# The sums of squares at six stage entries: summed by GpSimd in SBUF, or by TensorE in PSUM

## The chip, the core and the metric

The kernel runs on one core of a Trainium2 chip. The metric is the device time of one execution in microseconds (us), as the median of several. Lower is better. Everything is float32. TensorE (PE in the profile) multiplies, GpSimd (POOL), VectorE (DVE) and ScalarE (ACT) work elementwise, and the SP queue issues the weight DMAs.

## The reference, cut to what matters

The model is a chain of blocks on `x`, 512 tokens of width 1024: a mixer (convolution and attention), an MLP, a conformer convolution, a second MLP, and then a layer of another kind (forgetting attention and a gated feed-forward part). Six of its stages begin in the same way, with a root-mean-square norm of the running `x`, and a product of the normed `x` with a weight:

```python
def rms_norm(x, g):
    xf = x.astype(jnp.float32)
    y = xf * lax.rsqrt(jnp.mean(xf * xf, axis=-1, keepdims=True) + EPS)
    return (y * g.astype(jnp.float32)).astype(x.dtype)

for i in range(DEPTH):                       # DEPTH = 2
    h = rms_norm(x, g[0])                    # entries x0 (i = 0) and x2 (i = 1)
    m = parallel_conv_mla(h, ...) if i % 2 == 0 else conformer_conv(h, ...)
    x = x + rms_norm(m, g[1])
    h = rms_norm(x, g[2])                    # entries x1 and x3
    x = x + rms_norm(squared_relu_mlp(h, mlp_w1[i], mlp_w2[i]), g[3])
# second layer kind: n1 = _rmsnorm(h, norm1_w) is entry x4, n2 = _rmsnorm(h, norm2_w) is entry x5
```

## The kernel before

**Layout.** `x` lies transposed in SBUF: `X[:, k]` is k-tile k, 128 of the 1024 features on the partitions and the 512 tokens along the free dimension, k = 0 to 7. A float32 product is made of three products of fp32r parts: ScalarE rounds an operand to a high part (`XH`, `wh`), and another engine subtracts that from the original to get the low part (`XL` on VectorE, `wl` on GpSimd). `products` issues three matmuls: high x high, high x low, low x high. A weight block holds 8 tiles of 128x128 in a ring of 4 blocks; its chain is DMA, ScalarE `hi`, GpSimd `lo_range`, TensorE.

**The norm is applied afterwards.** A stage multiplies its weight with gain times `X`, not yet normed. Each output tile is multiplied with `r2`, the row of 1/rms factors of the 512 tokens, when VectorE takes it out of PSUM. So the products of an entry can start as soon as the first k-tile of the new `X` is there, and the factor is only wanted later. No output tile of a stage leaves PSUM before `r2` is ready, and TensorE can run four output tiles ahead at most (four PSUM banks, `bank_free`).

**An entry on TensorE** (`enter`, line 1475). The first three output tiles, t = 0 to 2, are computed together, one k-tile at a time: for each k TensorE waits for `xh` and `xl` of that k-tile, and issues 9 matmuls of 512 columns. (Entry x0 takes k = 0 to 3 for t = 0, then for t = 1, then for t = 2, and is k by k from k = 4.) Then comes the fourth output tile, t = 3, with two hooks: `stat` ahead of its k = 1 and `spread` ahead of its k = 5. `stat` (line 1433) sums the squares over the partitions: for each of four groups of 128 tokens it takes that 128x128 piece of `ssq` as the stationary operand and one column of ones as the moving one. These are float32 matmuls, which the profile shows as two each: 8 weight loads and 8 matmuls of one column. ScalarE takes the root (`root`, line 585), VectorE the reciprocal (`factor`), TensorE spreads it over the partitions (`spread`), and ScalarE copies it to `r2` (`keep_r2`).

**An entry on ScalarE** (`operand`, line 598). For each k: wait for the new `X[:, k]`, write `XH[:, k]` (line 610), then the square of `X[:, k]`: for k = 0 into `ssq` (line 614), for k >= 1 into `sqb[:, k % 2]` (line 619). The square of k-tile k waits until GpSimd has added that of k - 2, since it goes into the same half of `sqb`. ScalarE's queue is in order, so `XH[:, k + 1]` stands behind that wait, and the first weight block that is rounded after the entry stands behind all of them.

**An entry on VectorE** (`operand`, line 935). At x1 to x4, for each k: `update(k)` makes the new `X[:, k]` in two operations, and then `split(k - 1)` makes `XL[:, k - 1]`, once `XH[:, k - 1]` is there. At x0 and x5 `X` is there already, and only the splits are done.

**An entry on GpSimd** (`add_squares`, line 455). For k = 1 to 7 it waits for the square and adds `sqb[:, k % 2]` to `ssq` (line 462). This stands in GpSimd's one queue between two low parts of weight blocks: at x0 between the blocks 2 and 3, at the others behind the fourth block of the stage.

**Weight blocks around the entry.** The first four blocks of a stage are in the ring before the entry begins (at x0 the first three and, behind the additions, the fourth). Block 4 can be rounded when the first output tile is done with its block.

Of the kernel before, what the change touches and what calls it, by code (L numbers as in the profile page):

```python
# [31 lines left out]
P = 128  # L32
# [63 lines left out]

SSQ_ADDS = [sum(t - (name[0] == "x") for name, t, _ in _JOBS[:i + 1]) for i in range(len(_JOBS))]
JOB_D = [d for _, _, d in _JOBS]
# [30 lines left out]
def build(nc, x_t, meta_t, positions, vectors, weights, out_t):  # L129
    ctx = ExitStack()  # L130
    with ctx:
# [133 lines left out]
        xl = sem("xl")  # L265
        squares = sem("squares")
        ssq_adds = sem("ssq_adds")
        stat_done = sem("stat_done")
# [135 lines left out]
        def _(pool):  # L404
# [49 lines left out]

            def add_squares(entry):

                before = SSQ_ADDS[JOB[entry]] - (KT - 1)
                for k in range(1, KT):
                    pool.wait_ge(squares, SQUARES[entry] + k + 1)
                    if before + k - 1:  # L460
                        pool.wait_ge(ssq_adds, before + k - 1)
                    pool.tensor_tensor(ssq[:], ssq[:], sqb[:, k % 2], ALU.add).then_inc(ssq_adds, 1)  # L462

            for n in range(3):
                pool.wait_ge(w_hi, n + 1)
                pool.tensor_tensor(wl[:, n], raw[:, n], wh[:, n].bitcast(F32), ALU.subtract).then_inc(w_lo, 1)
            add_squares("x0")
            lo_range(3, 5)
# [10 lines left out]
            lo_range(BLOCK0["w_out"] + 4, BLOCK0["mlp0_up0"] + 4)  # L479
            add_squares("x1")  # L480
            lo_range(BLOCK0["mlp0_up0"] + 4, n0 + 4)
            add_squares("x2")
            done = n0 + 4

# [47 lines left out]
            lo_range(done, BLOCK0["mlp1_up0"] + 4)  # L532
            add_squares("x3")
            lo_range(BLOCK0["mlp1_up0"] + 4, BLOCK0["w_in_2"] + 4)
            add_squares("x4")

# [7 lines left out]
            lo_range(BLOCK0["w_out_2"] + 4, BLOCK0["ffn_up"] + 4)  # L544
            add_squares("x5")
            lo_range(BLOCK0["ffn_up"] + 4, NBLK)
# [3 lines left out]
        def _(sc):  # L550
# [47 lines left out]
            def operand(entry, blocks={}):  # L598

                o = OPN[entry]  # L600
                for k in range(KT):
                    for n in blocks.get(k, ()):
                        hi(n)
                    if entry == "x0":
                        sc.wait_ge(x_in[k], 16)
                    elif entry == "x5":
                        sc.wait_ge(bank_free, TILE0["w_out_2"] + k + 1)
                    else:
                        sc.wait_ge(x_new, KT * (R2N[entry] - 1) + k + 1)
                    sc.activation(XH[:, k], X[:, k], ACT.Copy, scale=ENTRY_GAIN[entry](k)).then_inc(xh, 1)  # L610
                    if k == 0:
                        if JOB[entry]:
                            sc.wait_ge(stat_done, JOB[entry])
                        sc.activation(ssq[:], X[:, 0], ACT.Square).then_inc(squares, 1)
                        continue
                    added = SSQ_ADDS[JOB[entry]] - (KT - 1) + max(k - 2, 0)
                    if added:
                        sc.wait_ge(ssq_adds, added)
                    sc.activation(sqb[:, k % 2], X[:, k], ACT.Square).then_inc(squares, 1)  # L619
# [269 lines left out]
        def _(v):  # L889
# [45 lines left out]
            def operand(entry):  # L935
# [20 lines left out]
                else:  # L956
                    for k in range(KT):
                        split(k)
                ssq_n[0] += KT - 1
                factor(entry)  # L960
# [449 lines left out]
        def _(pe):  # L1410
# [22 lines left out]
            def stat(job):  # L1433
# [10 lines left out]
                ins.then_inc(stat_done, 1)  # L1444

            def spread(job):

# [27 lines left out]
            def enter(phase, operand, hook_job=None):  # L1475
# [5 lines left out]
                for i, (k, t) in enumerate(order):  # L1481
# [7 lines left out]
                    if k == KT - 1:  # L1489
                        ins.then_inc(blocks_done, 1)  # L1490
                hooks = {1: lambda: stat(hook_job), 5: lambda: spread(hook_job)} if hook_job else {}
                tile(n0 + 3, T0 + 3, hooks)
# [454 lines left out]
```

## Time and profile before

| | us |
|---|---|
| median of 3 runs | 2103.38 |
| the lowest of them | 2101.74 |
| the highest of them | 3156.57 |
| span of the profiled execution | 2101.5 |

The two lower runs agree within 1.7 us, and the highest is an outlier that nothing of the kernel explains. The profile has one execution, whose span is 2101.5 us from its first to its last instruction; the median lies 1.9 us above that. Times in the rows further down are microseconds from the start of that span. In a row of the timeline the second number is how long the instruction or the group of merged instructions took; matmuls overlap, so the distance between two starts is what a matmul costs in a stream. The page counts TensorE as busy for 93% of the span, VectorE for 55%, ScalarE for 27% and GpSimd for 45%.

### The profile page before, as it was taken

To read this page: it belongs to the slowest core of one execution; us is meant where nothing else is said; L and a number is where in the kernel's file an instruction comes from. 1 tells how busy PE (TensorE), PEld (TensorE's weight loads), DVE (VectorE), ACT (ScalarE), POOL (GpSimd) and SP (SyncE) were. 2 spreads that over 40 slices of the span, in tenths; PEclk is the share of its full clock that TensorE was granted. 3 is DMA by queue.
4 is the path that set the end of the run, shared out by engine and by line. 5 is a ranking of instruction groups with operands and counts; after the bars stand their busy time and mean duration, and the time that the engine had idled before them with its cause. 6 is when DMAs were issued, how large, how long until landed. Compare 5 with 4: busy or idle time off the path is not lost.

```text
span 2101.5 us, 23925 instructions
## 1 busy us (share of the span) xinstructions
PE 1945.6 (93%) x8603; PEld 1586.4 (75%) x8603; DVE 1156.4 (55%) x1326; ACT 562.0 (27%) x822; POOL 938.4 (45%) x470
## 2 busy tenths in 40 slices
PE   7898999999999866669999999999999999999999
PEld 5777877788887645457787888878777777888887
DVE  4886577604845799987781285357332316444300
ACT  4226422112112321233311122133132224222221
POOL 6354445344444556744543444442221135444443
PEclk9999999999999987879999999999975599999999
DMA  4141022222222011112122223211100022322332
GB/s 170 47 135 60 13 68 91 88 93 100 93 97 80 33 49 58 60 41 80 61 91 89 91 99 100 92 59 52 60 31 1 1 70 80 100 91 98 100 101 79
DMA packets 46676, 157.80 MB, mean 75 GB/s; under 512 B 6544, under 2 KB 6800, under 8 KB 46608
## 3 DMA queue, kind: packets, MB, share of 16 engines
q1 hardware_dynamic: 46608, 156.86, 22.7%
q8 instruction: 46, 0.75, 0.1%
q14 instruction: 22, 0.18, 0.0%
HBM read 152.58 MB, written 2.10 MB: 74 GB/s over the span
## 4 chain that ended last, share of the span: by engine, by line
PE 71%; DVE 25%; issue 1%; ACT 1%; DMA 0%; DVEq 0%; POOL 0%; SPq 0%; ACTq 0%; POOLq 0%
PE PS L1413 22%; PE PS L1415 21%; PE PS L1414 21%; DVE acc L912 8%; DVE tmp L912 3%; DVE HL L904 2%; DVE tmp L904 2%; PE PS L1423 2%; DVE HH L1166 2%; DVE XL L912 2%; DVE X L904 1%; PE PS L1572 1%; DVE ssq L904 1%; DVE sqb L904 1%; PE PS L1589 1%
## 5 line engine op out<-in xcount | busy, mean ns | idle before, releaser
L432 POOL TENSOR_TENSOR wl<-raw,wh 128x1024 fp32r<-128x1024 f32 x244 | 602.7, 2472 | 794.7 <-ACT wh L579 487.5
L1413 PE MATMUL PS<-XH,wh 128*128 128x512 f32 x1440 | 576.9, 401 | 39.8 <-DVE XL L912 23.7
L1414 PE MATMUL PS<-XL,wh 128*128 128x512 f32 x1440 | 567.1, 394 | 0.0
L1415 PE MATMUL PS<-XH,wl 128*128 128x512 f32 x1440 | 566.6, 393 | 0.0
L1413 PEld LDWEIGHTS PS<-XH,wh 128*128 128x128 f32 x1440 | 274.5, 191 | 110.3 <-issue 38.8
L579 ACT ACTIVATE wh<-raw 128x1024 fp32r<-128x1024 f32 x152 | 161.1, 1061 | 669.0 <-PE PS L1415 669.0
L1415 PEld LDWEIGHTS PS<-XH,wl 128*128 128x128 f32 x1440 | 274.1, 190 | 58.9
L1414 PEld LDWEIGHTS PS<-XL,wh 128*128 128x128 f32 x1440 | 274.5, 191 | 54.1
L1413 PE MATMUL PS<-HH,wh 128*128 128x512 f32 x688 | 269.8, 392 | 8.4 <-DVE HL L904 8.4
L1414 PE MATMUL PS<-HL,wh 128*128 128x512 f32 x688 | 269.5, 392 | 0.0
L1415 PE MATMUL PS<-HH,wl 128*128 128x512 f32 x688 | 269.1, 391 | 0.0
L912 DVE SCALAR_TENSOR_TENSOR acc<-U,vec,acc 128x512 f32<-128x512 f32 x128 | 175.1, 1440 | 0.3
L904 DVE TENSOR_TENSOR tmp<-PS,r 128x512 f32<-128x512 f32 x126 | 86.7, 690 | 138.4 <-PE PS L1415 114.4
L1413 PEld LDWEIGHTS PS<-HH,wh 128*128 128x128 f32 x688 | 130.1, 189 | 36.3 <-POOL wl L432 9.2
L1414 PEld LDWEIGHTS PS<-HL,wh 128*128 128x128 f32 x688 | 130.3, 189 | 27.3
L1415 PEld LDWEIGHTS PS<-HH,wl 128*128 128x128 f32 x688 | 130.3, 189 | 27.1
L565 ACT ACTIVATE wh<-raw 128x1024 fp32r<-128x1024 f32 x94 | 98.5, 1055 | 189.6 <-PE PS L1415 174.1
L453 POOL TENSOR_TENSOR prob<-prob,cols 128x512 f32<-128x512 f32 (+2 forms) x64 | 57.4, 899 | 135.4 <-DVE cols L1100 135.4
L1166 DVE CAST HH<-tmp 128x512 f32 x64 | 110.1, 1721 | 9.6 <-DVE tmp L912 5.8
L1183 DVE COPY M<-PS 128x512 f32 x16 | 11.1, 691 | 159.1 <-PE PS L1415 159.1
L1095 DVE TENSOR_REDUCE cols<-PS 128x1 f32<-128x512 f32 (+2 forms) x64 | 38.2, 596 | 105.5 <-PE PS L1573 86.7
L462 POOL TENSOR_TENSOR ssq<-ssq,sqb 128x512 f32<-128x512 f32 x42 | 67.0, 1596 | 62.3 <-ACT sqb L619 60.6
(265 smaller groups left out, 2447.2 us busy)
## 6 DMA issues: line engine op xcount, KB each, us to landing
raw<-weights SPq DMA_DIRECT2D x286, 512.0 KB, 3.5
X<-x_t SPq DMA_DIRECT2D x8, 256.0 KB, 7.2
out_t<-X SPq DMA_DIRECT2D x8, 256.0 KB, 4.7
KH<-rope_h SPq DMA_DIRECT2D x4, 128.0 KB, 4.4
KL<-rope_l SPq DMA_DIRECT2D x4, 128.0 KB, 5.4
QH<-XH SPq DMA_DIRECT2D x16, 32.0 KB, 2.0
QL<-XL SPq DMA_DIRECT2D x16, 32.0 KB, 2.0
pos_i<-positions SPq DMA_DIRECT2D x1, 256.0 KB, 8.3
```

Source lines behind the costliest of these rows:

```text
L432: pool.tensor_tensor(wl[:, j], raw[:, j], wh[:, j].bitcast(F32), ALU.subtract).then_inc(w_lo, 1)
L453: pool.tensor_tensor(p, p, cols[:, u % 4, 2:3].broadcast_to(p.shape), ALU.mult).then_inc(p_done, 1)
L462: pool.tensor_tensor(ssq[:], ssq[:], sqb[:, k % 2], ALU.add).then_inc(ssq_adds, 1)
L565: sc.activation(wh[:, j], raw[:, j], ACT.Copy).then_inc(w_hi, 1)
L579: sc.activation(wh[:, j], raw[:, j], ACT.Copy).then_inc(w_hi, 1)
L904: return v.tensor_tensor(out, a, b, op)
L912: return v.scalar_tensor_tensor(out=out, in0=a, scalar=s, in1=b, op0=op0, op1=op1)
L1166: v.tensor_copy(HH[:, g * 4 + j], tmp[:, 1]).then_inc(dve, 1)
L1413: pe.matmul(out, wa, xa, start=start, stop=False)
L1414: pe.matmul(out, wa, xb, start=False, stop=False)
L1415: return pe.matmul(out, wb, xa, start=False, stop=stop)
L1423: pe.matmul(out, ident_r[:], ident_r[:].unsqueeze(1).broadcast_to((P, out.shape[-1] // P, P)), start=True, stop=True)
```

## The change

The squares of all eight k-tiles now go to the two halves of `sqb`, and `ssq` is not used at an entry. TensorE sums each k-tile's square over the partitions as soon as it has issued that k-tile's and the next k-tile's products: `sum_squares(entry, k - 1)` stands behind t = 2 of k-tile k (at x0 behind t = 0). The four columns of the statistics bank `PS[:, STAT, 0:4]` are accumulated over k: the first matmul of the first k-tile opens the accumulation, and the last k-tile closes it. The eighth sum, of k-tile 7, stands in the hook of the fourth output tile where `stat` stood. A new semaphore, `squares_summed`, tells ScalarE that a half of `sqb` has been read. The other norms (`m1` to `m4`, `ln`, the latents) keep `ssq` and `stat`.

```diff
-SSQ_ADDS = [sum(t - (name[0] == "x") for name, t, _ in _JOBS[:i + 1]) for i in range(len(_JOBS))]
+SSQ_ADDS = [sum(t * (name[0] != "x") for name, t, _ in _JOBS[:i + 1]) for i in range(len(_JOBS))]
...
+        squares_summed = sem("squares_summed")
...
-            def add_squares(entry):
-
-                before = SSQ_ADDS[JOB[entry]] - (KT - 1)
-                for k in range(1, KT):
-                    pool.wait_ge(squares, SQUARES[entry] + k + 1)
-                    if before + k - 1:
-                        pool.wait_ge(ssq_adds, before + k - 1)
-                    pool.tensor_tensor(ssq[:], ssq[:], sqb[:, k % 2], ALU.add).then_inc(ssq_adds, 1)
-
...
-            add_squares("x0")
             lo_range(3, 5)
...
             lo_range(BLOCK0["w_out"] + 4, BLOCK0["mlp0_up0"] + 4)
-            add_squares("x1")
             lo_range(BLOCK0["mlp0_up0"] + 4, n0 + 4)
-            add_squares("x2")
...
-            add_squares("x3")
             lo_range(BLOCK0["mlp1_up0"] + 4, BLOCK0["w_in_2"] + 4)
-            add_squares("x4")
...
             lo_range(BLOCK0["w_out_2"] + 4, BLOCK0["ffn_up"] + 4)
-            add_squares("x5")
             lo_range(BLOCK0["ffn_up"] + 4, NBLK)
...
                     sc.activation(XH[:, k], X[:, k], ACT.Copy, scale=ENTRY_GAIN[entry](k)).then_inc(xh, 1)
-                    if k == 0:
-                        if JOB[entry]:
-                            sc.wait_ge(stat_done, JOB[entry])
-                        sc.activation(ssq[:], X[:, 0], ACT.Square).then_inc(squares, 1)
-                        continue
-                    added = SSQ_ADDS[JOB[entry]] - (KT - 1) + max(k - 2, 0)
-                    if added:
-                        sc.wait_ge(ssq_adds, added)
+                    if k < 2 and JOB[entry]:
+                        sc.wait_ge(stat_done, JOB[entry])
+                    if k >= 2:
+                        sc.wait_ge(squares_summed, (KT - 1) * R2N[entry] + k - 1)
                     sc.activation(sqb[:, k % 2], X[:, k], ACT.Square).then_inc(squares, 1)
...
-                ssq_n[0] += KT - 1
                 factor(entry)
...
+            def sum_squares(entry, k):
+
+                n = JOB[entry]
+                if k == 0 and n:
+                    pe.wait_ge(sd_done, n)
+                pe.wait_ge(squares, SQUARES[entry] + k + 1)
+                for j in range(4):
+                    ins = pe.matmul(PS[:, STAT, j:j + 1], sqb[:, k % 2, j * P:(j + 1) * P], ones[:, 0:1],
+                                    start=k == 0 and j == 0, stop=k == KT - 1, skip_group_check=True)
+                ins.then_inc(stat_done if k == KT - 1 else squares_summed, 1)
+
...
                     if k == KT - 1:
                         ins.then_inc(blocks_done, 1)
-                hooks = {1: lambda: stat(hook_job), 5: lambda: spread(hook_job)} if hook_job else {}
+                    if hook_job and t == (0 if operand == "x0" else 2) and k >= 1:
+                        sum_squares(hook_job, k - 1)
+                hooks = {1: lambda: sum_squares(hook_job, KT - 1), 5: lambda: spread(hook_job)} if hook_job else {}
                 tile(n0 + 3, T0 + 3, hooks)
```

## Rows read from the trace of the kernel before

**Rows 1.** Page, costliest groups: busy us, mean ns | idle before, releaser.
```profile
L462 POOL TENSOR_TENSOR ssq<-ssq,sqb 128x512 f32<-128x512 f32 x42 | 67.0, 1596 | 62.3 <-ACT sqb L619 60.6
```
**Rows 2.** Timeline, entry x1, TensorE: start us, us, instruction [idle before, releaser].
```profile
303.59 0.39 PE L1413 MATMUL PS<-XH,wh 128*128 128x512 f32 x1
...
311.26 0.47 PE L1413 MATMUL PS<-XH,wh 128*128 128x512 f32 x1 [0.78 <-DVE XL L912]
...
321.22 0.39 PE L1413 MATMUL PS<-XH,wh 128*128 128x512 f32 x1
...
323.94 0.94 PE L1443 MATMUL PS<-ones,ssq 128*128 128x1 f32 x8
...
327.61 1.05 PE L1455 MATMUL PS<-ident,rcol 128*128 128x128 f32 x8
```
**Rows 3.** Timeline, entry x1: two splits on VectorE.
```profile
301.83 0.74 DVE L912 SCALAR_TENSOR_TENSOR XL<-X,vec,XH 128x512 fp32r<-128x512 f32 x1
...
303.88 1.79 DVE L912 SCALAR_TENSOR_TENSOR XL<-X,vec,XH 128x512 fp32r<-128x512 f32 x1
```
**Rows 4.** Timeline, entry x1: the first addition on GpSimd.
```profile
303.27 1.85 POOL L462 TENSOR_TENSOR ssq<-ssq,sqb 128x512 f32<-128x512 f32 x1 [9.73 <-ACT sqb L619]
```
**Rows 5.** Timeline, entry x1: high part and square of k-tile 1 on ScalarE.
```profile
301.95 0.72 ACT L610 ACTIVATE XH<-X,vec 128x512 fp32r<-128x512 f32 x1
302.58 0.62 ACT L619 ACTIVATE sqb<-X 128x512 f32<-128x512 f32 x1
```
**Rows 6.** Timeline, TensorE: first product and statistics matmuls of entries x2, x3, x4.
```profile
676.73 0.47 PE L1413 MATMUL PS<-XH,wh 128*128 128x512 f32 x1
...
697.93 0.95 PE L1443 MATMUL PS<-ones,ssq 128*128 128x1 f32 x8
...
1003.61 0.39 PE L1413 MATMUL PS<-XH,wh 128*128 128x512 f32 x1
...
1024.21 0.95 PE L1443 MATMUL PS<-ones,ssq 128*128 128x1 f32 x8
...
1378.57 0.39 PE L1413 MATMUL PS<-XH,wh 128*128 128x512 f32 x1
...
1398.70 0.95 PE L1443 MATMUL PS<-ones,ssq 128*128 128x1 f32 x8
```
**Rows 7.** Timeline, TensorE: the same two of entry x5.
```profile
1735.34 0.77 PE L1413 MATMUL PS<-XH,wh 128*128 128x512 f32 x1 [4.28 <-DVE XL L912]
...
1753.81 0.95 PE L1443 MATMUL PS<-ones,ssq 128*128 128x1 f32 x8
```
**Rows 8.** Timeline, entry x0: TensorE.
```profile
15.43 0.77 PE L1413 MATMUL PS<-XH,wh 128*128 128x512 f32 x1 [1.16 <-DVE XL L912]
...
17.11 0.76 PE L1413 MATMUL PS<-XH,wh 128*128 128x512 f32 x1
...
18.52 0.63 PE L1413 MATMUL PS<-XH,wh 128*128 128x512 f32 x1
...
34.12 0.95 PE L1443 MATMUL PS<-ones,ssq 128*128 128x1 f32 x8
```
**Rows 9.** Timeline, entry x0: weight block 3 on ScalarE and GpSimd.
```profile
23.75 1.04 ACT L565 ACTIVATE wh<-raw 128x1024 fp32r<-128x1024 f32 x1
...
26.28 2.40 POOL L423 TENSOR_TENSOR wl<-raw,wh 128x1024 fp32r<-128x1024 f32 x1
```
**Rows 10.** Timeline, TensorE at the slow clock: the statistics matmuls of `m1`.
```profile
294.14 1.68 PE L1443 MATMUL PS<-ones,ssq 128*128 128x1 f32 x8 [2.08 <-DVE ssq L904]
```
**Rows 11.** Timeline, TensorE in stage `w_in_2`: matmuls of 16 columns among the products.
```profile
1409.66 0.17 PE L1413 MATMUL PS<-meta_h,wh 128*128 128x16 f32 x1
...
1410.25 0.48 PE L1413 MATMUL PS<-XH,wh 128*128 128x512 f32 x1
...
1411.02 0.17 PE L1413 MATMUL PS<-meta_h,wh 128*128 128x16 f32 x1
```
**Rows 12.** Busy time by stretch: us, then PE, PEld, DVE, ACT, POOL busy (count), PEclk, DMA share, GB/s.
```profile
1410.00:1416.00 6.00, 6.00 (x42) 5.49 (x42) 1.90 (x4) 0.00 (x0) 0.00 (x0) 1.00 0.33 122
```

## The prediction

> **What bounds the kernel now.** I read the page's groups first, then the timelines of the six entries, engine by engine. The page gives the size of what goes: 42 GpSimd additions of 1.6 us, 67.0 us of work, and the idle time before them is GpSimd waiting for squares [rows 1]. That GpSimd waits for ScalarE, and not the other way round, says that the additions are seldom late. So the question is who paces an entry.
>
> At x1 the first product is at 303.59 and the statistics matmuls are at 323.94 [rows 2]. In between lie 8 k-tiles x 9 products and the 3 of the fourth tile's k = 0: 75 products in 20.35 us. A product costs 0.2267 us in an unbroken stream: the 12 from 321.22 to 323.94 take 2.72 us [rows 2]. 75 of them make 17.00 us, so TensorE waits 3.35 us in this entry, and the wait is for VectorE's `XL` [rows 2]. VectorE is late since it does not run at its own pace. A split that begins with GpSimd idle takes 0.74 us; the one from 303.88 takes 1.79 us, and the first addition had GpSimd from 303.27 to 305.12 [rows 3, 4]. The additions thus cost the entry time, but through VectorE. At its free pace VectorE needs 2.05 us per k-tile (303.88 - 301.83), TensorE 9 x 0.2267 = 2.04. So what the change can give back at x1 is bounded by those 3.35 us.
>
> **What it removes.** The additions, 67.0 us of GpSimd's time, all off the path but for the splits that they stretch. That returns at most what TensorE waits at each entry. By the distance from first product to statistics, less 17.00:
>
> - x1: 20.35, waits 3.35 [rows 2]
> - x2: 21.20, waits 4.20 [rows 6]
> - x3: 20.60, waits 3.60 [rows 6]
> - x4: 20.13, waits 3.13 [rows 6]
> - x5: 18.47 [rows 7]. Its surplus of 1.47 is the slow clock of the first products (the first takes 0.77 us, others 0.39): TensorE waits for nothing, and the additions cost nothing here.
>
> The square at k = 0 went to `ssq` and now goes to `sqb`: same operation, 0.62 us [rows 5], no change.
>
> **What it adds.** Per entry, `stat` becomes eight sums, each the same four matmuls as `stat`; the eighth stands where `stat` stood. So each entry gets seven more, 42 in all. Their price is in the trace, in the same surroundings: from 323.94 to 327.61 there are the statistics matmuls and 12 products [rows 2]. 3.67 - 2.72 = 0.95 us for a sum, the weight loads and the slower restart of the products included. It is nearly all weight loading: one column is multiplied, and 128x128 loaded, eight times over. From the row's first start, 8 matmuls x 0.10 us; I take the whole 0.95.
>
> Here the Trainium skill has another price. "TensorE: Matmul & The Clock Gate", section "Back-to-back issue gap", gives about 81 ns per matmul for a sustained stream of weight loads and matmuls of 128 columns. Eight of those are 0.65 us, by which the 39 sums at full clock would cost 11.7 us less in all. The row of this trace does not agree, and it is the same instruction, so the row decides.
>
> **TensorE becomes the bound of x1 to x4.** A k-tile now costs it 2.04 + 0.95 = 2.99 us, against VectorE's 2.05. So the waits are gone, and seven sums stand in their place: 7 x 0.95 = 6.65.
>
> - x1: 6.65 - 3.35 = +3.30
> - x2: 6.65 - 4.20 = +2.45
> - x3: 6.65 - 3.60 = +3.05
> - x4: 6.65 - 3.13 = +3.52
> - x5: nothing to give back, +6.65
>
> That makes +12.3 for x1 to x4, and +19.0 with x5. If VectorE stayed as slow as it is, its 2.72 us per k-tile (20.35 / 7.5) would still be under 2.99, so this does not hang on the contention being gone.
>
> **Entry x0.** The first sum falls into the wait of 1.16 us ahead of k = 2 [rows 8] and what remains of the gap. TensorE has the slow clock there: products are 0.43 us apart. A sum at that clock takes at most 1.68 us, from the statistics of `m1` [rows 10]; I take 1.6. Sum 0 then ends at about 15.65, 0.2 after the start of k = 2 in the trace (15.43). k = 2 and k = 3 cost 1.41 each (17.11 to 18.52 [rows 8]), sums 1 and 2 cost 1.6 each: the tile t = 1 starts at 15.65 + 2.82 + 3.2 = 21.7 in place of 18.52, +3.15. From 18.52 to 34.12 there are 63 products in 15.60 us, of which 14.28 are at full clock and 1.3 are the slow clock's [rows 8]. Sums 3 to 6 add 4 x 0.95 = 3.8. If the clock rises when it does now, the 1.3 are saved, +5.6. If its rise comes as much later as the stream does, +6.9. If the sums hold it back by twice that delay, half of the second 3.15 is lost too, +8.5. I take +6.8.
>
> A second wait appears at x0. ScalarE rounds weight block 3 behind its last square, and that square now waits for sum 5. From the end of sum 5 to the fourth tile TensorE has 9 products, sum 6 and 6 products: 2.04 + 0.95 + 1.36 = 4.35 us. Square, rounding and low part take 0.62 + 1.04 + 2.40 = 4.06, and some 0.3 in hops [rows 5, 9]. It is a tie that costs 0.5 at most. At the other entries only block 4 stands there, which is wanted a whole tile (24 products, 5.4 us) later.
>
> **The new loop.** The square of k waits for the sum of k - 2, which ends where TensorE begins k. Behind it on ScalarE stands `XH` of k + 1, and behind that on VectorE the split of k + 1. From the start of k: 0.62 + 0.72 + 0.74 = 2.08, with hops about 2.3 [rows 3, 5]. TensorE wants it after 2.99, so 0.7 us hide it.
>
> **Moved besides.** GpSimd's memsets of `CQ` and `CK` (line 540) stood behind the additions of x4 and now come before the entry, where GpSimd is idle (9.73 us before the first addition of x1 [rows 4]); they may stretch a VectorE operation once, up to 1 us, bound from the split that took 1.79 for 0.74. No DMA moves, and no weight block waits for an addition at x1 to x5.
>
> **Nothing gives it back.** Everything behind an entry waits for `r2`, which comes from the last sum, through root, reciprocal and spread as before. The statistics come later by the sums above, and so does all that follows.
>
> **Sum.** 12.3 + 6.65 + 6.8 = +25.8 us: a span of 2101.5 + 25.8 = 2127.3, and 1.9 above it as before, a time of 2129. That is 1.2% slower, inside the 2% (42 us) that a measurement of this kernel tells from no change.
>
> **Rivals.**
> 1. *Cheaper sums.* Weight loads could slip under running products more than they do around `stat`. At 0.65 us each the total is 25.8 - 39 x 0.30 = +14, 2117. For it: only the rule above. Against it: `stat` too has an unbroken stream of products on both sides, and costs 0.95 [rows 2]. 9 in 100.
> 2. *The loop decides.* If hops make the loop longer than 2.99 us, each us over costs 6 k-tiles x 5 entries = 30 us. At 3.5 us: +15, so +41 and 2144. Against it: 0.7 us of room. 7 in 100.
> 3. *Slower by more than 2%: the clock.* Sums of one column fill 0.95 of 2.99 us, 32% of an entry. If TensorE fell to half clock there, a product would cost 0.43 for 0.23 and a sum 1.6 for 0.95: 72 x 0.2 + 7 x 0.65 = 19 us for an entry. One whole entry at half clock makes +45, which is where 2% is passed; all six make about +140, 2243. Against it: in stage `w_in_2`, six matmuls of 16 columns take 0.59 of each 1.36 us (1409.66 to 1410.25, next 1411.02), 43% of the time, and the granted clock of that stretch is 1.00 [rows 11, 12]. Also the waits of x1, 16% of it, did not bring it down. 5 in 100. The Trainium skill's page "TensorE: Matmul & The Clock Gate", Part 1, says that the slow clock is the default and activity lifts it, which is why it is a rival at all.
> 4. *No net change.* If the splits now free of GpSimd gave more than TensorE's waits, or `r2` came no later, the time would stay at 2103. Against it: 42 more sums stand in TensorE's own stream, 40 us of them, and the waits are 14.3. 3 in 100.
>
> **How the numbers follow.** The likeliest case, 76 in 100, is 2129, and its own range is 2120 to 2138: below, a sum of 0.81 (8 matmuls x 0.10) and +5.6 at x0, 12.3 - 3.9 + 5.7 + 5.0 = +19; above, 1.7 and 0.5 more at x0, 1 for the memsets, and some 5 of my own doubt about hops and the clock. To hold 8 in 10 with some of rivals 1 and 2 it becomes 2115 to 2142. Slower by over 2% (above 2145): rival 3 and a piece of rival 2, 0.06. Faster by over 2%: no case, 0.01. Within 2%: 0.93.
>
> **What would show it.** In the changed kernel's timeline of x1: splits of 0.74 us all through; no wait on `XL` behind k = 0; products of a k-tile and then 8 matmuls of one column; about 23.65 us from first product to last sum for 20.35. The same at x2 to x4, 25.1 at x5. At x0 the last sum near 41. The prediction is wrong if a sum costs much under 0.95, if TensorE waits for ScalarE or VectorE inside an entry, or if the granted clock falls there.

## The result, and the profile after

The changed kernel takes 2129.11 us (median of 4 runs, 2121.88 to 2130.97), the kernel before 2102.56 beside it. The ratio is 1.0127, 95% interval 1.0101 to 1.0152: 26.6 us slower, where the prediction said 2129 and +25.8. Single runs far above the others (3156.57 among the four of the kernel before, 2472.68 and 4115.92 among the seven of e2 below) are outliers, and the ratios leave them out. The profiled execution took 2130.97 us, its span 2129.2.

The page of the changed kernel: span, busy time by engine, and the chain's shares.

```profile
span 2129.2 us, 24514 instructions
...
PE 1981.1 (93%) x8939; PEld 1629.0 (77%) x8939; DVE 1134.6 (53%) x1326; ACT 562.5 (26%) x822; POOL 872.2 (41%) x428
...
PE 76%; DVE 21%; issue 1%; ACT 1%; DVEq 0%; DMA 0%; POOL 0%; SPq 0%; ACTq 0%; POOLq 0%
```

TensorE has 336 matmuls more than in the kernel before (8603), which is 42 sums of 8. GpSimd has 42 operations less and 66.2 us less to do (938.4 before), VectorE 21.8 us less (1156.4) for the same 1326 instructions. TensorE's share of the chain went from 71 to 76%, VectorE's from 25 to 21%. So GpSimd and VectorE got lighter, and TensorE, which now sets the pace in every entry, got heavier.

The timeline of entry x1 on TensorE (start us, us, instruction), which answers to [rows 2]. L1394 is the high x high product, the first of each three, and L1434 a sum.

```profile
311.06 0.47 PE L1394 MATMUL PS<-XH,wh 128*128 128x512 f32 x1
...
315.32 0.95 PE L1434 MATMUL PS<-ones,sqb 128*128 128x1 f32 x8
316.13 0.48 PE L1394 MATMUL PS<-XH,wh 128*128 128x512 f32 x1
...
318.29 0.95 PE L1434 MATMUL PS<-ones,sqb 128*128 128x1 f32 x8
319.10 0.47 PE L1394 MATMUL PS<-XH,wh 128*128 128x512 f32 x1
...
334.75 0.95 PE L1434 MATMUL PS<-ones,sqb 128*128 128x1 f32 x8
```

No row of the entry carries a wait any more. A k-tile takes 318.29 - 315.32 = 2.97 us (predicted 2.99). From first product to last sum it is 334.75 - 311.06 = 23.69 us, for 20.35 in the kernel before (predicted 23.65).

The same entry on VectorE: the splits are 0.75 us long, where one took 1.79 before [rows 3], and the wait stands in front of VectorE now (in brackets: idle before, and who ended it).

```profile
317.58 0.75 DVE L894 SCALAR_TENSOR_TENSOR XL<-X,vec,XH 128x512 fp32r<-128x512 f32 x1 [1.19 <-ACT XH L596]
...
320.55 0.75 DVE L894 SCALAR_TENSOR_TENSOR XL<-X,vec,XH 128x512 fp32r<-128x512 f32 x1 [0.84 <-ACT XH L596]
```

The same entry on ScalarE, which answers to [rows 5]. The square waits for the sum of two k-tiles earlier, and the next `XH` stands behind it.

```profile
316.30 0.63 ACT L601 ACTIVATE sqb<-X 128x512 f32<-128x512 f32 x1 [3.25 <-PE PS L1434]
316.84 0.71 ACT L596 ACTIVATE XH<-X,vec 128x512 fp32r<-128x512 f32 x1
```

This is the loop of the prediction: TensorE begins its k-tile at 316.13, the square starts at 316.30, `XH` at 316.84, the split at 317.58 and is done at 318.33. TensorE wants it at 319.10. So 0.77 us of room, as against the 0.7 that was forecast.

Busy time by stretch (us, then PE, PEld, DVE, ACT, POOL busy with counts, PEclk, DMA share, GB/s): all of x1, and x5 cut in two at 1761.1.

```profile
311.00:334.70 23.70, 23.67 (x132) 20.41 (x132) 13.10 (x19) 9.17 (x15) 1.53 (x1) 1.00 0.00 1
...
1755.00:1761.10 6.10, 6.05 (x14) 4.79 (x15) 1.22 (x2) 0.00 (x0) 0.00 (x0) 0.50 0.30 86
1761.10:1781.50 20.40, 20.40 (x118) 17.74 (x117) 3.76 (x5) 9.20 (x13) 1.54 (x1) 1.00 0.00 1
```

TensorE is busy all through x1 (23.67 of 23.70) and the granted clock is 1.00 there. x2 to x4 read the same. At x5 the first 14 products run at 0.50, before any sum has been made, and from the first sum on at 1.00. In the column PEclk, 1.00 means the faster of the two clock levels and 0.50 the slower one; a value between them is the mean of a stretch that holds both.

The other two entries on TensorE, x0 and x5, which answer to [rows 7, 8]:

```profile
14.33 1.70 PE L1434 MATMUL PS<-ones,sqb 128*128 128x1 f32 x8
15.89 0.77 PE L1394 MATMUL PS<-XH,wh 128*128 128x512 f32 x1
...
21.86 0.77 PE L1394 MATMUL PS<-XH,wh 128*128 128x512 f32 x1
...
27.13 0.45 PE L1394 MATMUL PS<-XH,wh 128*128 128x512 f32 x1
...
42.52 0.95 PE L1434 MATMUL PS<-ones,sqb 128*128 128x1 f32 x8
...
1755.05 0.77 PE L1394 MATMUL PS<-XH,wh 128*128 128x512 f32 x1 [4.27 <-DVE XL L894]
...
1762.11 0.95 PE L1434 MATMUL PS<-ones,sqb 128*128 128x1 f32 x8
...
1781.54 0.95 PE L1434 MATMUL PS<-ones,sqb 128*128 128x1 f32 x8
```

By entry, first product to last sum (at x0 the start of the last sum), in us:

| entry | before | after | measured | predicted |
|---|---|---|---|---|
| x0 | 34.12 | 42.52 | +8.40 | +6.8 |
| x1 | 20.35 | 23.69 | +3.34 | +3.30 |
| x2 | 21.20 | 23.52 | +2.32 | +2.45 |
| x3 | 20.60 | 23.63 | +3.03 | +3.05 |
| x4 | 20.13 | 23.52 | +3.39 | +3.52 |
| x5 | 18.47 | 26.49 | +8.02 | +6.65 |
| between and behind them | | | -0.80 | 0 |
| span | 2101.5 | 2129.2 | +27.7 | +25.8 |

### The profile page after: what moved, and what is told of

Read it like the earlier page. It is cut to its first block, busy times and chain, and to the rows that moved or that the text cites. A ratio compares the mean times of both kernels' runs of the same rounds, so it can differ in the third digit from the quotient of the medians.

```text
span 2129.2 us, 24514 instructions
## 1 busy us (share of the span) xinstructions
PE 1981.1 (93%) x8939; PEld 1629.0 (77%) x8939; DVE 1134.6 (53%) x1326; ACT 562.5 (26%) x822; POOL 872.2 (41%) x428
## 4 chain that ended last, share of the span: by engine, by line
PE 76%; DVE 21%; issue 1%; ACT 1%; DVEq 0%; DMA 0%; POOL 0%; SPq 0%; ACTq 0%; POOLq 0%
PE PS L1394 23%; PE PS L1396 22%; PE PS L1395 22%; DVE acc L894 8%; PE PS L1404 2%; DVE tmp L894 2%; DVE HL L886 2%; PE PS L1434 2%; DVE tmp L886 2%; DVE HH L1147 2%; PE PS L1566 1%; DVE ssq L886 1%; DVE sqb L886 1%; PE PS L1583 1%; PE PS L1578 1%
## 5 line engine op out<-in xcount | busy, mean ns | idle before, releaser
L1394 PE MATMUL PS<-XH,wh 128*128 128x512 f32 x1440 | 579.9, 403 | 31.1 <-DVE XL L894 15.6
L1394 PEld LDWEIGHTS PS<-XH,wh 128*128 128x128 f32 x1440 | 275.2, 191 | 91.3 <-issue 23.2
L1394 PE MATMUL PS<-HH,wh 128*128 128x512 f32 x688 | 270.2, 393 | 8.4 <-DVE HL L886 8.4
L1394 PEld LDWEIGHTS PS<-HH,wh 128*128 128x128 f32 x688 | 130.5, 190 | 36.3 <-POOL wl L433 9.2
L1164 DVE COPY M<-PS 128x512 f32 x16 | 11.1, 692 | 159.9 <-PE PS L1396 159.9
L1394 PE MATMUL PS<-UH,wh 128*128 128x512 f32 x64 | 31.5, 492 | 64.5 <-DVE tmp L886 48.7
```

Of the source, the lines that this page charges most:

```text
L1394: pe.matmul(out, wa, xa, start=start, stop=False)
```

## Experiments

All kernels are the kernel before with a mode for each entry: additions on GpSimd as before, sums on TensorE as in the change, or one of the variants below. Three groups ran, each with its own runs of the kernel before: e1 to e4 (2102.02 us), e5 to e8 (2102.41), e9 to e11 (2100.90). The edits shown are shortened to the lines that matter. The theory is the prediction's: a sum costs TensorE 0.95 us, and all that the change gives back is what VectorE's stretched splits made TensorE wait at x1 to x4. Its rivals are cheaper or dearer sums, the loop over ScalarE, and the clock.

**The change in two halves, e1 and e2.** The new sums at x1 to x4 only, then at x0 and x5 only.

```diff
+MODE = {x0: "G", x1: "T", x2: "T", x3: "T", x4: "T", x5: "G"}   # e1; e2 the other way round
-    hooks = {1: lambda: stat(hook_job), ...}
+    hooks = {1: lambda: sum_squares(hook_job, KT - 1) if MODE[hook_job] == "T" else stat(hook_job), ...}
```

> The change at the entries x1 to x4 alone; x0 and x5 keep GpSimd's additions. By my theory (7 sums of 0.95 us in TensorE's stream, less the waits for VectorE that they take the place of) x1 to x4 cost +3.3, +2.45, +3.05 and +3.5: +12.3 over the kernel before, about 2115 us. Rival, the GpSimd additions stretched nothing and a sum costs its full price everywhere: 28 x 0.95 = +26.6, 2129. Rival, the sums fall into TensorE's waits: about 0, 2103.

> The change at the entries x0 and x5 alone, where TensorE had no wait for VectorE to give back. My theory: +6.65 at x5 and +6.8 to +8.4 at x0 (the more, the later the slow clock ends), +13.5 to +16.5 in all, about 2117 us. Rival, the loss comes from the loop over ScalarE at x1 to x4: then these two entries cost next to nothing, 2103 to 2106.

e1: 2114.38 us, ratio 1.0059 (1.0036 to 1.0082), +12.4 where +12.3 was predicted; its entries x1 to x4 take 23.69, 23.52, 23.55 and 23.53. e2: ratio 1.0056 (1.0035 to 1.0077). The median of its seven runs, 2117.27, includes the two outliers; the other five have the median 2112.77, +10.8, which is below the +13.5 to +16.5 that was expected. The halves then make +23.1, the whole +26.6: they add up within their intervals, of 4 to 5 us each. The times can't tell whether the four entries or the two cost more. By the traces x1 to x4 of e1 cost +12.0, and the two ends of e2 +13.9 (x0 ends at 41.57, x5 takes 24.95): 14 sums cost more than 28, since only at the four was a wait to be given back.

The trace of e2 also shows how much the same code differs from one execution to the next. Its entries x1 to x4, which are those of the kernel before, take 21.22, 20.77, 20.08 and 21.13, for 20.35, 21.20, 20.60 and 20.13 there.

**Without the additions, e3.** The squares are still made, the factor comes from k-tile 0 alone, so the rest of the sum of squares is left out. This asks whether the additions held VectorE up, and what that was worth.

```diff
             def add_squares(entry):
+                if MODE[entry] != "G":           # "N" at all six entries
+                    return
...
             def stat(job):
                 pe.wait_ge(ssq_adds, SSQ_ADDS[n])
+                if MODE.get(job) == "N":
+                    pe.wait_ge(squares, SQUARES[job] + KT)
```

> The kernel before, with the seven additions per entry left out (the squares are still computed; the norm's factor at each entry is then taken from k-tile 0 alone, so the output is another). It measures what the additions themselves cost. My theory: they cost time only by stretching VectorE at x1 to x4, where TensorE's waits of 3.35, 4.20, 3.60 and 3.13 us nearly go: each entry falls to 17.0 to 17.5 us, and the total by 12 to 14, to about 2090 us; every split takes 0.74 us. Rival, the splits are long for another reason (ScalarE's accesses or VectorE's own queue): splits of 1.79 stay, and the time is 2103.

2084.78 us, ratio 0.9923 (0.9895 to 0.9951). Entry x1 of this kernel on TensorE, first product and statistics matmuls:

```profile
303.28 0.39 PE L1446 MATMUL PS<-XH,wh 128*128 128x512 f32 x1
...
320.28 0.95 PE L1478 MATMUL PS<-ones,ssq 128*128 128x1 f32 x8
```

and two splits that follow each other on VectorE, where [rows 3] had 0.74 and 1.79:

```profile
303.58 0.75 DVE L942 SCALAR_TENSOR_TENSOR XL<-X,vec,XH 128x512 fp32r<-128x512 f32 x1
...
305.63 0.75 DVE L942 SCALAR_TENSOR_TENSOR XL<-X,vec,XH 128x512 fp32r<-128x512 f32 x1
```

The entry takes 17.00 us, to the hundredth the 75 products x 0.2267 that the prediction took as the floor, and VectorE's period is the 2.05 that it took as the free pace. x2 to x4 take 17.29, 17.00 and 17.25. The waits that come back are 3.35, 3.91, 3.60 and 2.88, 13.7 us in all, against the prediction's 14.3. The expected 2090 was missed by 5: the medians differ by 17.2, the entries by 13.7. The rest of the trace's difference lies between x3 and x5 (3.8 us shorter than in the kernel before). That part varies by itself: from the last sum of x4 to the first product of x5 it is 331.6 to 338.0 us over the traces. 13.7 is inside the interval (10 to 22 us).

How an addition holds VectorE up can be read from the trace of the kernel before, together with [rows 3, 4]:

```profile
305.32 1.49 POOL L462 TENSOR_TENSOR ssq<-ssq,sqb 128x512 f32<-128x512 f32 x1 [0.20 <-ACT sqb L619]
305.59 0.73 DVE L912 SCALAR_TENSOR_TENSOR tmp<-M,vec,PS 128x512 f32<-128x512 f32 x1
306.36 1.00 DVE L904 TENSOR_TENSOR X<-X,tmp 128x512 f32<-128x512 f32 x1
```

The operation on `X` and `tmp` ends at 307.36, 0.55 us after the addition's end at 306.81. The split of [rows 3] ends at 305.67, also 0.55 us after its addition [rows 4]. At x1 to x4 the 12 splits and the 12 updates of `X` that begin when an addition is already under way end 0.54 to 0.56 us after it. The operation from 305.59, which reads one of its inputs from PSUM, takes its usual 0.73 us in the middle of an addition. So these VectorE operations with two inputs in SBUF don't run more slowly: they wait for the addition's end. Every second k-tile pays 1.79 - 0.74 = 1.05 us for the split and 0.31 for the update of `X`, which is 0.68 per k-tile. 2.05 + 0.68 is within 0.01 of the 2.72 per k-tile of the kernel before.

**Each sum twice, e4.** Four more float32 matmuls behind each of the 48 sums, into columns that nobody reads.

```diff
+                for j in range(4, 8):
+                    ins = pe.matmul(PS[:, STAT, 64 + j:65 + j], sqb[:, k % 2, (j % 4) * P:(j % 4 + 1) * P], ones[:, 0:1], start=False, ...)
```

> The changed kernel with each of the 48 sums made twice, the second time into columns nobody reads. It prices the sum. My theory: 0.8 to 0.95 us for each second sum at full clock, 1.6 at the slow clock for three of them: 48 x 0.81 + 2.4 = 41 to 48 x 0.95 + 2 = 48 us over the changed kernel, 2170 to 2177 us. Rival, weight loads slip under products once they stand in a longer row (0.65 each): +31, 2160. Rival, the loop over ScalarE sets the pace: a second sum makes no difference until it is longer than that loop: under +20.

2183.03 us, ratio 1.0387 (1.0364 to 1.0410), which is 54 over the changed kernel and more than the 41 to 48 expected. Behind the last sums of x1, on TensorE:

```profile
350.31 1.02 PE L1492 MATMUL PS<-ones,sqb 128*128 128x1 f32 x8
351.20 1.85 PE L1495 MATMUL PS<-ones,sqb 128*128 128x1 f32 x8
352.91 0.77 PE L1446 MATMUL PS<-XH,wh 128*128 128x512 f32 x1
```

and the stretch behind them by windows:

```profile
352.90:357.40 4.50, 4.50 (x12) 3.53 (x13) 0.18 (x1) 1.12 (x2) 2.37 (x1) 0.50 0.06 22
```

The second sums cost 0.89 each: the entry is 6.24 us longer than the 23.69 of the changed kernel, for 7 of them (the eighth's comes behind the point that is measured). 48 x 0.89 = 42.7. The rest is the clock. Behind the last sums of x1 to x5 the granted clock is 0.50 for a while. From the eighth sum to the spread the five entries take 7.73, 6.12, 6.13, 6.14 and 7.73 us, where x0, without such a spell, takes 4.55: 11.1 us in all. Together that is 53.8 of the 54. So the theory of the sums holds, and the rival of the clock is real at twice the sums. In the changed kernel no stretch of x1 to x5 behind the first sum has it; at x0 the slow pace lasts longer, as shown below.

**Twice but for the last, e11.** If the crowd of 32 matmuls of one column with only three products among them brings the clock down, the fall should go with the eighth sum made once.

```diff
-                for j in range(4, 8):
+                for j in range(4, 8 if k < KT - 1 else 4):
```

> As e4, but the eighth sum of each entry is made once. In e4 the granted clock was 0.50 for about 4.5 us behind the last sums of x1 and x5, where 32 matmuls of one column had only three products between them, and the same shows at x2 to x4. Theory A, that crowd of sums brought the clock down: now it stays at full speed, and the seven second sums cost 42 x 0.89 + 2 = 39 us over the changed kernel, 2168 us. Theory B, the sums' share of the whole entry (45%) brought it down: the slow spells stay, some 2 us for each entry more, about 2178 us.

2173.74 us, ratio 1.0353 (1.0331 to 1.0374), between the two numbers. The stretches behind the last sum of x1 and of x2 by windows:

```profile
347.70:352.10 4.40, 4.40 (x14) 3.50 (x14) 0.18 (x1) 1.13 (x2) 2.37 (x1) 0.61 0.40 119
732.70:735.50 2.80, 2.80 (x14) 2.33 (x14) 0.18 (x1) 1.13 (x2) 1.43 (x1) 1.00 0.63 187
```

The spell is gone at x2 and x4 and still there at x1, x3 and x5. The 0.61 at x1 is the mean of 8 products at the slow level (11 in e4) and some at full speed. From the eighth sum to the spread the five entries take 5.22, 3.65, 5.23, 3.66 and 5.22 us, where 3.66 is the time without a spell: 4.7 us of slow clock, for 11.1 in e4. The medians lie 9.3 us apart and the profiled executions 12.2, of which six sums are 5.3 and the clock 6.4. Neither answer fits alone: the crowd takes part, and what else decides stays open. There is one trace of each kernel, and how much a spell differs between executions of one kernel isn't known.

**The additions left running for nothing, e5.** The sums are TensorE's, and GpSimd also makes seven operations of the old shape at x1 to x5, that no one needs. If the splits' stretch still mattered in the new kernel, it would show.

```diff
+                for k in range(1, KT):
+                    pool.wait_ge(squares, SQUARES[entry] + k + 1)
+                    pool.tensor_tensor(ssq[:], ssq[:], ssq[:], ALU.subtract)
```

> The changed kernel, and GpSimd makes its seven additions of the kernel before at x1 to x5 all the same, gated by the same squares, on values nobody reads. It asks whether the stretched VectorE still matters once the sums are in TensorE's stream. My theory: splits are stretched again (some at 1.8 us), but a k-tile costs TensorE 2.99 us and VectorE 2.72 at most, so the time stays that of the changed kernel, 2129 us, or up to 3 us more. Rival, VectorE and the loop over ScalarE are near the bound and each stretch shows: 4 entries x 7 k-tiles x some 0.5 us, +14, 2143.

2127.74 us, ratio 1.0115 (1.0098 to 1.0132): the changed kernel's time. Two splits of x1 on VectorE, the second k-tile's and a later one:

```profile
313.19 1.53 DVE L943 SCALAR_TENSOR_TENSOR XL<-X,vec,XH 128x512 fp32r<-128x512 f32 x1
...
319.29 1.02 DVE L943 SCALAR_TENSOR_TENSOR XL<-X,vec,XH 128x512 fp32r<-128x512 f32 x1 [1.14 <-ACT XH L631]
```

and the idle addition on GpSimd that ran beside the first of them:

```profile
312.58 1.59 POOL L469 TENSOR_TENSOR ssq<-ssq 128x512 f32<-128x512 f32 x1 [7.62 <-ACT sqb L638]
```

The splits are stretched again, to 1.02 to 1.53 us, and again each ends 0.55 us after GpSimd's operation; but TensorE's period stays 2.97: at 2.97 per k-tile there is room for it. The load is lighter than the old one, since these operations read `ssq` alone and take 1.04 us in the median, where the additions took 1.55; splits of 1.79 were not tried against the new sums. Only the first k-tiles, where no sum stands yet, get longer: x1 takes 24.43 for 23.69, x2 to x4 0.4 to 0.8 more. That small part doesn't show in the median.

**Sums with fewer weight loads, e6.** Squares and ones rounded to fp32r: four matmuls of two columns in place of eight of one.

```diff
-    ins = pe.matmul(PS[:, STAT, j:j + 1], sqb[:, k % 2, j * P:(j + 1) * P], ones[:, 0:1], ...)
+    ins = pe.matmul(PS[:, STAT, 2 * j:2 * j + 2], sqr[:, k % 2, j * P:(j + 1) * P], ones_r[:, 0:2], ...)
```

> The changed kernel, with the squares and the ones in fp32r: each of the four matmuls of a sum is then one pass and not two, so 4 weight loads in place of 8 (two columns are multiplied in place of one). The squares are rounded, so the result is a little less exact. My theory, weight loads are the price: a sum falls from 0.95 to 0.45 to 0.55 us, 39 x 0.45 = 17 to 20 us less, and 2 to 3 less at the slow clock: about 2109 us; x1 to x4 at 17.0 + 7 x 0.5 = 20.5 us each. Rival, the price is the break of the stream and not the loads: 2125 us or more.

2109.37 us, ratio 1.0029 (1.0017 to 1.0042). TensorE at x1:

```profile
311.37 0.50 PE L1496 MATMUL PS<-ones_r,sqr 128*128 128x2 f32 x4
311.73 0.48 PE L1450 MATMUL PS<-XH,wh 128*128 128x512 f32 x1
...
313.90 0.50 PE L1496 MATMUL PS<-ones_r,sqr 128*128 128x2 f32 x4
```

A k-tile takes 2.53, of which 2.04 are products: a sum costs 0.49, and x1 to x4 take 20.54, 20.40, 20.45 and 20.40, where 20.5 was expected. Half the pairs of a weight load and a matmul, half the price, though each matmul has twice the columns. So the 0.95 goes by the number of such pairs and not by columns. Whether the load or the matmul of a pair sets its 0.12 us isn't separated by any run, since both were halved.

**One load of ones, e7 and e8.** The ones become the stationary operand, 128x128, and the rounded square moves through with 512 columns. The bank then holds the sum for every partition, so root and reciprocal work on 128x512 and the spread falls away. e7 at x1 to x3, e8 at all but x4.

```diff
+                if MODE[entry] == "F":
+                    pe.matmul(PS[:, STAT], ones_r[:], sqr[:, k % 2], start=k == 0, stop=k == KT - 1)
...
+                    sc.activation(r2[:], PS[:, STAT], ACT.Sqrt, bias=EPS, scale=1.0 / D)
...
+                    v.reciprocal(r2[:], r2[:])
```

> x1 to x3: the sum turned round. The ones (128x128, fp32r) are the stationary operand and the rounded square of 512 columns the moving one: one matmul per k-tile, and the sum comes out on all 128 partitions, so root and reciprocal are taken of 128x512 and give r2 without the spread through TensorE. x0, x4, x5 as in the kernel before. My theory: a sum costs one product, 0.23 us, the entry falls to 17.0 + 7 x 0.23 = 18.7 us from first product to last sum (before: 20.35, 21.20, 20.60), -5.9 in all, and the eighth sum and the spread are 1.65 us shorter at each, -5: about 2092 us, faster than the kernel before by 11. Rival, the longer root and reciprocal make r2 later and TensorE waits for banks: 2103 or more.

> As e7, at x0 and x5 too (x4 keeps GpSimd's additions, since a later step needs its factors by token). My theory: at x5 seven sums of 0.23 cost 1.6 and the shorter statistics give back 1.65; at x0 three sums at the slow clock cost 0.43 each and four 0.23, +2.2, less 1.65: within 1 us of e7, about 2092 us. Rival, without the additions and the spread these entries gain as well: 2088.

e7: 2092.65 us, ratio 0.9948 (0.9931 to 0.9965). e8: 2094.24, ratio 0.9972 (0.9958 to 0.9986). e7 at x1 on TensorE:

```profile
309.88 0.39 PE L1492 MATMUL PS<-sqr,ones_r 128*128 128x512 f32 x1
310.20 0.47 PE L1450 MATMUL PS<-XH,wh 128*128 128x512 f32 x1
...
312.35 0.39 PE L1492 MATMUL PS<-sqr,ones_r 128*128 128x512 f32 x1
```

and on VectorE:

```profile
309.30 0.75 DVE L946 SCALAR_TENSOR_TENSOR XL<-X,vec,XH 128x512 fp32r<-128x512 f32 x1 [1.24 <-ACT XH L633]
...
323.84 3.35 DVE L968 RECIPROCAL r<-r 128x512 f32<-128x512 f32 x1 [4.27 <-ACT r L607]
```

One full-width matmul costs about 0.25 us in place of 0.95. The entries take 19.30, 19.30 and 19.42, where 18.7 was expected: the periods alternate between 2.29 and 2.46, and the split waits for `XH`. That is the prediction's loop over ScalarE, of some 2.3 to 2.4 us, which begins to bind when TensorE's round is this short. By the traces the three entries give back 4.1 us, and the stretches from one entry to the next behind them 6.0 us, where the eighth sum is one matmul and the spread is gone. So more than half of e7's gain has nothing to do with the additions.

In e8 the wait that the prediction feared at x0 for weight block 3 appears, on TensorE:

```profile
34.71 0.50 PE L1450 MATMUL PS<-XH,wh 128*128 128x512 f32 x1 [0.48 <-POOL wl L431]
```

It gains no more than e7 though it has more of the cheap sums. That fits ends which have no wait to give back. Against e7, x0 ends 1.7 us later and the way from it to x1 is 2.1 shorter, x5 is 2.3 longer and the way behind it 0.9 shorter: about +0.9 in all, which is less than executions differ. No run took the ends alone in this form.

**The loop opened, e9 and e10.** ScalarE writes `XH` of k + 1 ahead of the square of k. e9 is e7 with that order, e10 is e1 with it.

```diff
                     sc.activation(XH[:, k], X[:, k], ...).then_inc(xh, 1)
-                    sc.activation(dst(k), X[:, k], ACT.Square)
+                    for i in ((k - 1,) if k < KT - 1 else (k - 1, k)):
+                        sc.activation(dst(i), X[:, i], ACT.Square)
```

> As e7, but ScalarE writes XH of k-tile k + 1 ahead of the square of k, so XH no longer stands behind the wait for a free half of sqb. In e7 a k-tile took 2.38 us in the mean (2.29 and 2.46 in turn), not 2.27, and TensorE started each just behind its split. My theory: that was the loop sum, square, XH, split, and without it TensorE runs at 2.04 + 0.23: 18.6 us per entry for 19.3, 2 us in all, about 2090.5 us. Rival, the 0.1 us is the cost of switching banks and operands: 2092.6 as e7.

> As e1 (the change at x1 to x4 alone), with the same swap of XH and square on ScalarE. In the changed kernel the loop over ScalarE is hidden by some 0.7 us, so my theory says no difference from e1: 23.6 us per entry, 2114 us. Rival, the loop costs a part of each 2.97 us: some 0.1 us x 7 x 4 = 3 us less, 2111.

e10: 2113.48 us, ratio 1.0064 (1.0043 to 1.0084), x1 23.62: no difference to e1, so the loop costs the change nothing. e9: 2089.06, ratio 0.9949 (0.9933 to 0.9965), x1 on TensorE:

```profile
309.55 0.39 PE L1495 MATMUL PS<-sqr,ones_r 128*128 128x512 f32 x1
309.78 0.40 PE L1453 MATMUL PS<-XH,wh 128*128 128x512 f32 x1
...
311.84 0.39 PE L1495 MATMUL PS<-sqr,ones_r 128*128 128x512 f32 x1
```

The period is a steady 2.29, the entries take 18.76, 18.85 and 18.76. So here the loop did bind, and was worth 0.4 to 0.7 us an entry; the ratios of e7 and e9 can't tell such a difference, the traces can. e9 has the lowest median of the kernels that compute the whole, 11.8 us under the kernel before.

## Why the prediction was right

**The bound and the waits.** TensorE waited for VectorE, and VectorE was late because of GpSimd: without the additions (e3) x1 takes 17.00 us, with splits of 0.75 us. The prediction had read both from single rows [rows 2, 3]. It did not see that the splits wait for the end of an addition.

**The price of a sum.** 0.95 taken; measured 0.93 (2.97 - 2.04) in the period. The rival of 0.65 us is out. The prediction put the price down to weight loading, which e6 does not separate from the matmuls. The figure behind the rival is that of the Trainium skill, "TensorE: Matmul & The Clock Gate", section "Back-to-back issue gap": about 81 ns per matmul in a stream of weight loads and matmuls of 128 columns. The matmuls of one column here don't reach it: in e4, with 16 of these matmuls in a row, the period of x1 is 3.86 us (343.97 to 347.83), so the 16 cost 3.86 - 2.04 = 1.82, or 0.114 us each.

**The entries x1 to x4.** +12.08 measured, +12.3 predicted, each within 0.13 us. The length after the change is what was forecast, 17.00 + 6.65 = 23.65, and it came out at 23.52 to 23.69. The length before is partly luck: the waits that were subtracted come from the very trace that the change is compared with, and the same code takes 20.08 to 21.23 us for an entry in other executions. TensorE now sets the pace, and e5 shows that it still does with splits of up to 1.53 us. That it would with the old splits, the step on 2.72 against 2.99, stays argued.

**Entry x0, mis-sized.** +8.40 for +6.8. The parts: the tile t = 1 starts at 21.86, 3.34 later than before (predicted 3.15), four sums at full clock are 3.80, and the remaining 1.26 are six products more at the slow pace. That is the text's third case, "if the sums hold it back by twice that delay" (+8.5), which it had named and not taken. The step that failed is the choice of +6.9's case. The starts of the first matmul at full pace, over all kernels:

| x0 has | full pace from |
|---|---|
| no sums on TensorE (e10, e9, e7, e3, before, e1) | 18.61, 20.63, 20.80, 20.98, 21.09, 21.60 |
| row sum, one full-width matmul (e8) | 19.43 |
| four matmuls of two columns (e6) | 23.45 |
| the change's sums (e2, after, e5) | 25.55, 27.13, 28.34 |
| each sum twice (e11, e4) | 30.16, 30.24 |

A full-pace product of e8 and one of e10, from their timelines of TensorE, and the stretch ahead of the rise in the changed kernel by windows (PEclk is the 1.00):

```profile
19.43 0.40 PE L1450 MATMUL PS<-XH,wh 128*128 128x512 f32 x1
...
18.88 0.39 PE L1449 MATMUL PS<-XH,wh 128*128 128x512 f32 x1
...
13.00:27.10 14.10, 14.10 (x45) 12.10 (x46) 4.80 (x4) 3.72 (x6) 1.99 (x1) 1.00 0.43 168
```

Their 0.40 and 0.39 us stand beside the 0.63 and 0.77 of the products at the slow pace. TensorE was busy without a gap in the changed kernel from 13.0 to 27.1, and still the pace rose only then. All six kernels without sums at x0 reach it by 21.60, all three with the change's sums from 25.55 on, and the two with twice as many last. So the sums ahead of the rise go with a later rise, and each there costs more than its 1.56 us (15.89 - 14.33). Executions of the same code at x0 lie 2.8 us (the change) and 3.0 us (without sums) apart, which bounds how well this can be forecast. Over the traces x0 ends at 32.52 to 34.75 without sums on TensorE and at 41.57 to 43.21 with the change's, in the mean 8.7 us later: the miss is not one execution's. The Trainium skill, "TensorE: Matmul & The Clock Gate", Part 1, says that activity lifts the slow clock. The trace does not bear that out by TensorE's busy time alone, since it was busy from 13.0 to 27.1 all through.

**Weight block 3 at x0.** A tie, as forecast. The fourth tile's next product starts at 41.83 and no wait is recorded; it takes the faster sums of e8 to make one, 0.48 us, the size the text had put on it.

**Entry x5, mis-sized.** +8.02 for +6.65. From the first sum on, all is as predicted: 1781.54 - 1762.11 = 19.43. Ahead of it 18 products take 7.06 us (1755.05 to 1762.11), where 4.08 is full pace: the slow clock holds for 14 products, some 1.4 us more than in the kernel before. No sum has been made by then. The same stretch took 5.51 in e2, 6.89 in e6, 5.55 in e8. In the six kernels whose x5 is without sums on TensorE the whole entry takes 18.45 to 19.46 (18.47 in the kernel before, at the low end), and with the change's sums 24.95, 26.33 and 26.49. So the surplus is how long the slow spell behind the attention stage lasts in an execution, and no sum of x5 has a part in it; e2's x5 is +6.48.

**The memsets** cost nothing that shows. The one of `CQ` runs at 1387.1, ahead of x4, and from the last sum of x3 to the first product of x4 it is 354.25 us for 354.36 before. e1, e2, e3, e5, e6 and e10 have 353.1 to 354.3 there, so 1 us could be hidden.

**What hid the two errors.** x0 and x5 are 3.0 over, x1 to x4 0.2 under, and 0.8 came back between the entries, mostly from x0 to x1 (-0.93) and x2 to x3 (-0.65), against +0.95 from x1 to x2. One such place can be seen: the statistics matmuls of `m1` took 1.68 at the slow clock before [rows 10] and 1.05 after. That is not the change's: e1 and e10, whose x0 is that of the kernel before, show 1.05 too. The way from x4 to x5, which differs by 6 us between executions, happens to be the same in both traces. That the time's +26.6 came within 1 us of the forecast is luck to that extent; its interval reaches from +21 to +32.

**The clock as rival.** Not at x1 to x5 of the changed kernel, where the granted clock is 1.00 from the first sum on. At x0 it took its part, the 1.26 us above, and e4 shows that it isn't far at the others: 54 in place of 42.7 with twice the sums.

## What to carry over

Ask first which engine sets the pace of the very stretch that is changed, and price what is moved onto it by the rows of that same instruction in such surroundings: here 42 times 0.95 us against 14.3 us of waits, before anything was built. Work of an engine off the path can still cost, when the engine that is late has to wait for its operations to end; taking it away pays only if what the bounding engine gets in its place is less than its waits. When TensorE is to sum over partitions, put the wide operand on the moving side and the ones on the stationary one: 0.25 us in place of 0.95. It paid twice in e7: where a wait stood to be given back (4.1 us), and behind the entries, where a short last sum and no spread let the factors come earlier (6.0 us).

## What the runs showed of the hardware

- A VectorE operation of 128x512 with two inputs in SBUF that begins during a GpSimd `TENSOR_TENSOR` of the same size ends 0.54 to 0.56 us after it: splits of 0.75 us become 1.02 to 1.79 (before, e5), and stay 0.75 with no addition there (e3). An operation that reads PSUM keeps its 0.73 us (before).
- A sum of matmuls with one or two columns, each with its own 128x128 weights, costs by their number: 0.95 us for 8, 0.49 for 4, 1.82 for 16. One matmul of 512 columns costs 0.25 (after, e6, e4, e9).
- At the start of the kernel full pace begins at 18.6 to 21.6 us without matmuls of one column ahead of it, at 25.6 to 28.3 with 24 of them, and at 30.2 with 48. With twice the sums the granted clock also falls to 0.50 behind the last of them at x1 to x5 (e4). The column of the granted clock reads 1.00 for 13.0 to 27.1 of the changed kernel, though the products there are 0.43 us apart; at the start of a kernel the pace of the products is what to read.
- A reciprocal of 128x512 takes VectorE 3.35 us, four and a half times a split (e7).
